# Latent attention: where the transposes, the dense products and the copies stand beside the exponentials

## The reference

```python
q = (rmsnorm(c_q, q_norm_g) @ w_uq).reshape(B, T, MLA_HEADS, MLA_NOPE + MLA_ROPE)
kv = (rmsnorm(c_kv, kv_norm_g) @ w_ukv).reshape(B, T, MLA_HEADS, MLA_NOPE + MLA_V)
...
# for each block of 128 query rows:
s = (jnp.einsum("bqhd,bkhd->bhqk", qn_b, k_nope)
     + jnp.einsum("bqhd,bkd->bhqk", qr_b, k_rope)).astype(jnp.float32) * scale
s = jnp.where(kpos[None, :] <= qpos[:, None], s, -jnp.inf)
p = jax.nn.softmax(s, axis=-1).astype(v.dtype)
return jnp.einsum("bhqk,bkhd->bqhd", p, v)
...
return o.reshape(B, T, MLA_HEADS * MLA_V) @ w_out
```

## Time and profile before

| | |
|---|---|
| time, median of 3 runs | 2194.67 us (2190.80 to 2196.29) |
| profiled execution, its own time | 2192.19 us |
| its span | 2190.4 us |
| PE busy | 2132.7 us, 97% of the span |
| POOL, DVE, ACT busy | 1218.3, 1133.1, 604.4 us |
| stretch of the latent units (scores of u = 0 to values of u = 15) | 883.2 to 999.2 us |

### The profile page before, as it was taken

The page is one execution under the profiler, slowest core; times in us unless marked ns, Lnnn a source line. Parts: engine busy times, 40 slices in busy tenths (PEclk is TensorE's granted clock), DMA queues, the critical chain, the costliest instruction groups (busy, mean ns, idle before and its releaser), DMA issues.

```text
span 2190.4 us, 29272 instructions
## 1 busy us (share of the span) xinstructions
PE 2132.7 (97%) x11912; PEld 1706.8 (78%) x11912; DVE 1133.1 (52%) x1571; ACT 604.4 (28%) x1234; POOL 1218.3 (56%) x687
## 2 busy tenths in 40 slices
PE   7999999999999999998999999999999999999998
PEld 5777777778888887767888888777777778887886
DVE  6566656477374564554321313477764464445333
ACT  4445445232021124342211202523332230012113
POOL 6433334477777775325566666654445366657663
PEclk9999999999999999999999999999999999999999
DMA  8322222255454542212233332222232132223331
GB/s 333 137 88 88 98 87 90 77 182 211 144 202 144 208 138 84 61 39 103 81 97 97 97 99 93 87 87 68 68 105 69 50 124 96 91 83 101 104 104 68
DMA packets 69139, 239.88 MB, mean 110 GB/s; under 512 B 6951, under 2 KB 12045, under 8 KB 68622
## 3 DMA queue, kind: packets, MB, share of 16 engines
q1 hardware_dynamic: 67388, 234.07, 31.2%
q10 hardware_dynamic: 1618, 3.94, 0.5%
HBM read 233.79 MB, written 4.19 MB: 109 GB/s over the span
## 4 chain that ended last, share of the span: by engine, by line
PE 91%; DVE 4%; ACT 2%; POOL 1%; issue 1%; DMA 0%; SPq 0%; ACTq 0%; DVEq 0%; POOLq 0%
PE bank L605 16%; PE bank L607 16%; PE bank L606 16%; PE bank L812 8%; PE bank L624 3%; PE bank L626 3%; PE bank L625 3%; PE mid L899 2%; PE mid L1411 1%; PE bank L641 1%; PE bank L643 1%; PE bank L642 1%; PE mid L649 1%; PE bank L866 1%; POOL wL L564 1%; PE bank L868 1%
## 5 line engine op out<-in xcount | busy, mean ns | idle before, releaser
L562 POOL TENSOR_SCALAR wH<-stage 128x1024 fp32r<-128x1024 f32 (+1 forms) x340 | 387.5, 1140 | 917.3 <-PE bank L607 260.8
L564 POOL TENSOR_TENSOR wL<-stage,wH 128x1024 fp32r<-128x1024 f32 (+1 forms) x340 | 832.1, 2447 | 28.4
L605 PE MATMUL bank<-hH,wH 128*128 128x512 f32 x944 | 368.6, 390 | 0.7 <-DVE A L2165 0.3
L607 PE MATMUL bank<-hH,wL 128*128 128x512 f32 x944 | 367.4, 389 | 0.0
L606 PE MATMUL bank<-hL,wH 128*128 128x512 f32 x944 | 367.3, 389 | 0.0
L605 PE MATMUL bank<-RA,wH 128*128 128x512 f32 (+1 forms) x756 | 274.4, 363 | 6.3 <-POOL wL L564 5.0
L607 PE MATMUL bank<-RA,wL 128*128 128x512 f32 (+1 forms) x756 | 272.8, 361 | 0.0
L606 PE MATMUL bank<-RA,wH 128*128 128x512 f32 (+1 forms) x756 | 272.6, 361 | 0.0
L605 PEld LDWEIGHTS bank<-hH,wH 128*128 128x128 f32 x944 | 177.2, 188 | 39.7 <-issue 3.3
L607 PEld LDWEIGHTS bank<-hH,wL 128*128 128x128 f32 x944 | 177.2, 188 | 37.0
L606 PEld LDWEIGHTS bank<-hL,wH 128*128 128x128 f32 x944 | 177.3, 188 | 36.6 <-issue 0.2
(11 more groups left out here) (421 smaller groups left out, 3532.8 us busy)
## 6 DMA issues: line engine op xcount, KB each, us to landing
WIDE<-in_ada_t SPq DMA_DIRECT2D x44, 1024.0 KB, 5.6
stage<-in_ffn_w_gate SPq DMA_DIRECT2D x44, 512.0 KB, 3.3
stage<-in_ffn_w_up SPq DMA_DIRECT2D x44, 512.0 KB, 3.3
stage<-in_c_wkv SPq DMA_DIRECT2D x32, 512.0 KB, 3.3
stage<-in_gdn_w_in SPq DMA_DIRECT2D x32, 512.0 KB, 3.3
stage<-in_ffn_w_down SPq DMA_DIRECT2D x32, 512.0 KB, 3.5
stage<-in_o_w_in SPq DMA_DIRECT2D x32, 512.0 KB, 3.2
stage<-in_e_w_in SPq DMA_DIRECT2D x26, 512.0 KB, 3.2
```

The source lines that it names most:

```text
L562: pool.tensor_scalar(high[:, 0:n], raw[:, 0:n], 1.0, 0.0, ALU.mult, ALU.add).then_inc(w_high, 1)
L564: pool.tensor_tensor(low[:, 0:n], raw[:, 0:n], high[:, 0:n].bitcast(F32), ALU.subtract).then_inc(w_split, 1)
L605: pe.matmul(bank[:, 0:n], h[:, k, c], xh[:, k, :], start=first and k == 0, stop=False)
L607: mm = pe.matmul(bank[:, 0:n], l[:, k, c], xh[:, k, :], start=False, stop=last and k == kc - 1)
```

## The change

Two orders are rewritten; no instruction is added or removed, and no semaphore changes.

On PE, `latent_pair` now runs scores of u, turn of u - 1, all the chunks in one run ((2, 5, 5, 5) for t = 0 to 3), values of u - 1. For the last pair this is the order that already stood there.

On ACT, each unit is now: copies of u - 1; at a pair's first unit `latent_y` of the pair before; exponentials of u; then the items' copies, none at t = 0, items 0 and 1 at t = 1, items 2 and 3 at t = 2, items 4, 5 and 6 at t = 3.

```diff
@@ latent_pair, PE @@
                     latent_scores(u)
-                    for part in range(2):
-                        if i < 3:
-                            n = ((2, 0), (3, 2), (3, 2), (3, 2))[t][part]
-                            latent(i + 1, range(at, at + n))
-                        else:
-                            n = ((0, 1), (0, 1), (0, 1), (0, 1))[t][part]
-                            for k in range(at, at + n):
-                                out_step("mla_out", k, k, 8 + k + 1)
+                    if u:
+                        latent_turn(u - 1)
+                    if i < 3:
+                        n = (2, 5, 5, 5)[t]
+                        latent(i + 1, range(at, at + n))
                         at += n
-                        if u:
-                            (latent_turn, latent_values)[part](u - 1)
+                    else:
+                        out_step("mla_out", t, t, 8 + t + 1)
+                    if u:
+                        latent_values(u - 1)
@@ ACT @@
-            for i in range(0, 4):
-                u = i * TT
+            for u in range(4 * TT):
+                i, t = divmod(u, TT)
+                if u:
+                    latent_copy(u - 1)
+                if i and t == 0:
+                    latent_y(i - 1)
                 latent_exp(u)
-                if i:
-                    latent_copy(u - 1)
-                    latent_y(i - 1)
                 if i < 3:
-                    latent_out(i + 1, 0)
-                latent_exp(u + 1)
-                latent_copy(u)
-                if i < 3:
-                    latent_out(i + 1, 1)
-                latent_exp(u + 2)
-                if i < 3:
-                    latent_out(i + 1, 2)
-                latent_copy(u + 1)
-                if i < 3:
-                    latent_out(i + 1, 3)
-                    latent_out(i + 1, 4)
-                latent_exp(u + 3)
-                latent_copy(u + 2)
-                if i < 3:
-                    latent_out(i + 1, 5)
-                    latent_out(i + 1, 6)
+                    for item in ((), (0, 1), (2, 3), (4, 5, 6))[t]:
+                        latent_out(i + 1, item)
```

## The result

The changed kernel takes 2201.32 us (median of 8 runs, 2198.69 to 2202.03), the kernel before 2193.51 in the same comparison; the ratio is 1.0031, 95% interval 1.0021 to 1.0041. That is 6.8 us slower (4.6 to 9.0) and within the range. The forecast was 4.0 us slower. The prediction took 0.3%, 6.6 us, for the least that a measurement of this kernel can tell from no change; the interval is narrower, about 2 us to either side, and leaves no doubt that the change costs time.

A forecast was written before the change was run, and what follows sets the result against it. PE, busy 97% of the span, was taken to bound the kernel. Taken away 6.7 us, added 4.9 + 0.8 + 4.6 = 10.3, so +3.6, rounded to +4.0: 2194.67 to 2198.7 us, range 2192.5 to 2204.5.

The forecast's parts named there:

- Taken away, 6.7 us: PE's six waits of the values for ACT's copies of the transposed probabilities go: 1.6 + 1.6 + 3.5 us.
- PE's order costs nothing: On PE, turns after the scores and one dense run cost nothing; no turn waits but the last.
- The pair's output ahead of the exponentials: At u = 4, 8, 12 the next scores wait 1.65 us each (4.9); item 0's later copy delays chunk 6 (0.8).
- Item 4 behind the exponentials of t = 3: In pairs 0 to 2, chunk 15 waits for the later copy of item 4: 1.5 us, three times, 4.6.
- POOL and DVE at u = 10: The scaling on DVE would start 0.1 us before POOL's L564, so the 1.9 us lost there would go.
- Rival 2: The meeting of POOL and DVE at u = 10 persists, chunk 15 waits 3.4 us: +5.9 us, 2200.6; chance 0.16.
- The sum: Over the changed stretch, added 10.3 less taken away 6.7 is +3.6, rounded up to +4.0 us, within 2.0 and 5.5.
- The clock as a sign of being wrong: The prediction is wrong if the granted clock in 883 to 1010 us falls below 1.00.
- Rival 1: The items' late copies don't reach PE at chunks 15 and 6: -1.8 us, 2192.9; chance 0.12.
- Rival 3: With rival 2, the clock also falls at the 3.4 us wait before chunk 15: +7.6 us, 2202.3; chance 0.09.
- Rival 4: Faster: the exponentials of t = 0 aren't held up by the pair's output; 2188 us; chance 0.03.

The follow-up runs named there:

- e4: PE's order of the changed kernel with ACT's order of the kernel before; 2196.62 us, ratio 1.0009 to the kernel before.
- e1: The changed kernel with the pair's output (`latent_y`) behind the exponentials of t = 0 instead of ahead; 2195.27 us, ratio 1.0007 to the kernel before.
- e2: The changed kernel with the copy of item 4 ahead of the exponentials of t = 3; 2195.55 us, ratio 1.0007 to the kernel before.
- e6: The changed kernel with POOL's second instruction on one slab cut to 64 of 1024 columns (output not the reference's); 2197.36 us, ratio 1.0016 to before.
- e8: The changed kernel with output behind, item 4 ahead, and POOL holding one slab until the negated maximum of u = 11; 2187.34 us, ratio 0.9968 to before.
- e3: The changed kernel with output behind the exponentials of t = 0 and item 4 ahead of those of t = 3; 2191.01 us, ratio 0.9989 to before.

## Why the prediction was right, and where not

- *Taken away, 6.7 us.* Right: no wait of the values for the copies is left. e4, which has the old ACT order, has all six. That the listed idle times of the six waits also add up to 6.7 is chance: the forecast's 6.7 is 7.7, reckoned from starts, less 0.95 for the scores of u = 14 and 15 and the last turn. Of this 0.95 only one wait of 0.47 us (u = 14) came.
- *PE's order costs nothing.* Nearly: 1.2 us in e4's stretch, of which 0.6 is a turn that waits because its scaling met POOL. In the changed kernel itself no turn waits, and the last one, put at 0.2 us, doesn't either.
- *The pair's output ahead of the exponentials.* Put at 1.65 us, three times, and 0.8 for item 0: 5.7 in all. The idle times are 1.39 us, three times, or 1.55 by starts; taking the order back (e1) gives 5.1 us in the stretch (120.5 - 115.4) and 5.3 by the ratios. The stall was right. The wait of chunk 6 for item 0 did not come: no wait at L1091 is listed behind u = 0, and in pair 1 chunk 6 starts 0.52 us behind the matmul before it (926.89 to 927.41), against 0.43 in e1.
- *Item 4 behind the exponentials of t = 3.* Put at 1.5 us, three times. Two of the three waits are 1.47 us, but some 0.3 to 0.4 of each is likely to be the scaling's meeting with POOL, which the forecast didn't have. e2 gives 4.3 us in the stretch back (120.5 - 116.2), and would give more but for the turn of u = 11.
- *POOL and DVE at u = 10.* This step failed, and it is the largest miss. The forecast let the 1.9 us go because the scaling would come first by 0.1 us. It came first by 0.09, and the delay stayed, since POOL's instruction then ran beside DVE's next one. The walk followed one pair of instructions instead of what DVE had queued behind it. Rival 2 had the right price and the right wait (3.4 forecast, 3.22 measured), though not the place, since it was the rotation and not the scaling that was held up; its chance of 0.16 was far too low. e6 shows the cause: without the long POOL instruction the wait falls from 3.22 to 1.18 us.
- *The sum.* +4.0 forecast, +5.9 with rival 2; 4.7 in the stretch, 6.8 (4.6 to 9.0) by the ratio. The stretch lies inside the forecast's own bounds of 2.0 and 5.5 partly by luck: the 2.0 us of POOL that were left out are offset in part by the 0.8 for item 0 and the half of 0.95 that did not come. The ratio lies above these bounds; the 2 us between the two go with a lower mean clock of the runs (0.9956 against 0.9963), and whether the change is what lowers it stays open.
- *The clock as a sign of being wrong.* The prediction called itself wrong if the granted clock in 883 to 1010 us fell below 1.00. It did: 0.57 over the 4 us from 892, behind the wait of 1.8 us at u = 1 that the prediction took to be harmless. One profile of the kernel before has the same fall, so the sign was badly chosen: it can't tell the two kernels apart.
- *The other rivals.* Rival 1, that the late items don't reach PE, is refuted by the waits at L1105, though it was right on chunk 6. Rival 3, the clock: its place was wrong, since through the wait of 3.22 us the granted clock stays at 1.00, and so was its rule that a single idle time between 1.8 and 3.8 us decides (below). Its time, +7.6, lies as near to the ratio's 6.8 as rival 2's 5.9. Rival 4, faster, did not come.

## What to carry to other kernels

Moving one class of work ahead on an in-order engine moves everything else back: list for each instruction that now stands later who waits for it, and from when. Here "copies ahead of the exponentials" was worth 6.7 us by the forecast's sum, and e8 shows as much in its stretch; two passengers of the same edit, the pair's output (5.1 us) and one item's copy (4.3), cost more than that; with these two put back, and PE's order and ACT's order changed together, the same idea is 7 us faster than before once POOL's slab is moved aside too (e8). A third passenger sits on no list of waits of the old kernel: the edit moves the times at which two other engines run, and new meetings of POOL and DVE came up at u = 2 and 6, at u = 10 with the rotation instead of the scaling, and in e2, e3 and e4 at u = 11. And two halves of an edit can't be judged one by one: alone they cost 2 and 18 us, together 7, while both are part of the fastest version.

## What the runs showed of the hardware

Where a DVE instruction with two inputs in SBUF starts while POOL's splitting (L564) runs, it ends 0.5 to 1.1 us behind POOL's end: 0.97 us became 2.90 before (POOL ends at 956.88, the scaling at 957.70), 0.68 became 2.84 in the changed kernel (967.83 and 968.37), and 1.23 became 3.03 in e8 (966.16 and 967.25). The Trainium skill (SBUF — State Buffer, section Who interferes with whom) says that a DVE instruction with two SBUF inputs contends with a POOL instruction that reads SBUF; these durations agree. What these runs add is that winning the race doesn't help when the next instruction on DVE is of the same kind. In the changed kernel, e1, e2, e3 and e4 the scaling of u = 10 came first and took 0.96 us, and the rotation's product right behind it took 2.84 or 2.85: POOL got in between the two.

After the same idle time of 1.8 us in the same code the granted clock fell in one profile of the kernel before (0.59 over 4 us) and not in the other (1.00). Behind the turn's wait of 2.3 us it fell in e3 and not in e2. It stayed at 1.00 through 3.22 us in the changed kernel: over 972 to 976 us, with PE busy for 0.78 of 4 us,

```profile
972.00:976.00 4.00, 0.78 (x7) 0.58 (x6) 2.38 (x5) 2.25 (x6) 0.00 (x0) 1.00 0.00 0
```

So in these profiles the length of the one idle time does not decide whether the 1.7 us are lost.
